# Two blocks, not three, for the experts loaded ahead of routing, and the overflow loop moved behind the 22nd expert

## What is computed

```python
def route(xt, w_router, router_bias):
    scores = jax.nn.sigmoid(jnp.dot(xt, w_router, preferred_element_type=jnp.float32))
    ...
    _, idx = lax.top_k(masked, TOP_K)          # 2 of 32 experts for each of 512 tokens
    w = jnp.take_along_axis(scores, idx, axis=-1)
    w = w / jnp.sum(w, axis=-1, keepdims=True)
    return idx, w

def moe(xt, idx, wts, w_gu, w_dn):
    ...
    def expert_block(args):
        xb, e = args
        g, u = jnp.split(xb @ w_gu[e], 2, axis=-1)
        return (jax.nn.silu(g) * u) @ w_dn[e]
    ...
    return jnp.einsum('tk,tkd->td', wts.astype(y.dtype), y)
```

## The kernel before, in words

| places | blocks each |
|---|---|
| 0 to 16 | 3 3 1 2 1 3 1 2 1 3 1 2 1 4 1 2 1 |
| 17 to 20 | 5 1 1 3 |
| 21 to 27 | 2 each |
| 28 to 31 | 1 each |

## Time and profile before

### The profile page before, as it was taken

How to read it: one execution, slowest core, us unless ns; L and a number is a source line. 1 busy time by engine, 2 the same in 40 slices (tenths; PEclk the granted TensorE clock), 3 DMA queues, 4 the chain that set the end, 5 groups by cost and what they waited for, 6 DMA issues and landing times.

```text
span 1829.8 us, 34673 instructions
## 1 busy us (share of the span) xinstructions
PE 1457.1 (80%) x14391; PEld 835.3 (46%) x14391; DVE 657.2 (36%) x1130; ACT 339.9 (19%) x776; POOL 309.1 (17%) x356
## 2 busy tenths in 40 slices
PE   3999999997985858997844999795787749888863
PEld 3644777566553424454422444344454325544431
DVE  5674777756110101111103289876311101111102
ACT  3344444111110001110102133301111001101000
POOL 1001111002221212322100111100232112222200
PEclk9998999986997979998977999896798879998976
DMA  9633222574899999999995122025699999999996
GB/s 368 241 153 147 84 80 73 160 284 190 336 393 403 404 402 363 381 408 407 411 404 216 46 75 84 3 92 230 244 371 382 408 423 358 396 409 397 415 420 243
DMA packets 89853, 517.14 MB, mean 283 GB/s; under 512 B 12859, under 2 KB 25556, under 8 KB 80242
## 3 DMA queue, kind: packets, MB, share of 16 engines
q1 hardware_dynamic: 76176, 497.96, 69.5%
q0 software_dynamic: 11616, 16.85, 2.9%
q10 hardware_dynamic: 1922, 0.29, 0.1%
HBM read 507.70 MB, written 22.02 MB: 289 GB/s over the span
## 4 chain that ended last, share of the span: by engine, by line
PE 50%; DMA 32%; DVE 11%; issue 4%; ACT 2%; SPq 1%; POOL 0%; POOLq 0%; DVEq 0%; ACTq 0%
DMA ring_gu<-in_moe_w_gu_dram 24%; PE ps L1055 15%; PE ps L1065 7%; DMA arena<-in_moe_w_gu_dram 4%; PE ps L857 3%; PE ps L972 3%; PE ps L748 3%; PE ps L884 3%; PE ps L937 2%; DVE ring_dn L1765 2%; PE ps L791 2%; PE ps L870 2%; PE ps L771 2%; PE ps L819 2%; DMA ring_gu<-in_w_ada_dram 1%
## 5 line engine op out<-in xcount | busy, mean ns | idle before, releaser
L1055 PE MATMUL ps<-ring_gu,arena 128*32 128x256 f32 x4992 | 337.4, 411 | 141.5 <-DMA ring_gu<-in_moe_w_gu_dram 92.3
L1986 DVE TENSOR_TENSOR arena<-arena,ps 128x128 f32<-128x128 f32 x120 | 34.5, 288 | 748.8 <-ACT arena L1407 748.8
L1055 PEld LDWEIGHTS ps<-ring_gu,arena 128*32 128x32 f32 x4992 | 169.9, 117 | 267.3 <-issue 94.2
L653 POOL DMA_INDIRECT ys_dram<-arena,out_idx x120 | 119.1, 992 | 750.4 <-DVE arena L1949 709.6
L1055 PE MATMUL ps<-arena 128*32 128x256 f32 x2688 | 182.7, 414 | 67.8 <-DMA arena<-in_moe_w_gu_dram 66.5
L1065 PE MATMUL ps<-ring_dn,arena 128*32 128x256 f32 x2496 | 169.6, 381 | 17.0 <-issue 13.6
L1055 PEld LDWEIGHTS ps<-arena 128*32 128x32 f32 x2688 | 90.9, 117 | 135.7 <-DMA arena<-in_moe_w_gu_dram 55.7
L1376 ACT ACTIVATE arena<-ps 128x128 f32<-128x128 f32 x120 | 33.3, 277 | 601.0 <-PE ps L1060 577.7
L646 POOL DMA_INDIRECT arena<-xn_dram,tok_idx x120 | 111.3, 927 | 116.9 <-issue 63.3
L1065 PEld LDWEIGHTS ps<-ring_dn,arena 128*32 128x32 f32 x2496 | 85.2, 110 | 85.8 <-issue 35.0
L937 PE MATMUL ps<-arena 128*128 128x512 f32 x256 | 110.6, 592 | 1.0 <-ACT arena L1189 1.0
(11 more groups left out here) (311 smaller groups left out, 1679.4 us busy)
## 6 DMA issues: line engine op xcount, KB each, us to landing
ring_gu<-in_moe_w_gu_dram SPq DMA_DIRECT2D x44, 4096.0 KB
ring_dn<-in_moe_w_dn_dram SPq DMA_DIRECT2D x44, 2048.0 KB
arena<-in_moe_w_gu_dram SPq DMA_DIRECT2D x20, 4096.0 KB
arena<-in_moe_w_dn_dram SPq DMA_DIRECT2D x20, 2048.0 KB
ring_gu<-in_w_ada_dram SPq DMA_DIRECT2D x12, 2048.0 KB, 20.4
ring_gu<-in_w_ada_dram SPq DMA_DIRECT2D x48, 512.0 KB, 3.6
arena<-in_rnn_w_in_dram SPq DMA_DIRECT2D x8, 1024.0 KB, 7.1
ring_dn<-ys_dram SPq DMA_DIRECT2D x8, 1024.0 KB, 7.9
```

What stands on the lines that cost most here:

```text
L653: g.indirect_dma_start(ys_dram, bass.IndirectOffsetOnAxis(ap=out_idx[:, col:col + 1], axis=0), yo[:, n % 4, :], None, bounds_check=2 * TIL ...
L1055: last = mm(ps[s_ * ROWS:(s_ + 1) * ROWS, pb, 0:2 * QF].rearrange("p (a b) -> p a b", a=2), rows[:, k, :], pair[:, :, s_, :], start=(k == ...
```

## The change

Experts 0 and 1 get two blocks instead of three (`CAP`, `FIXED`), and orders 18 and 19 get two blocks instead of one (`HEAVY` from 18 to 20), so that 60 blocks remain. `RUN` is written anew for these orders. The overflow loop moves from behind place 12 (block 23) to behind place 21 (block 43) and has 28 steps instead of 26. VectorE computes the new capacities with two more operations in each layer. Some small buffers in `arena` move to make room for two more columns. In the changed kernel the lines of the two products are L1056 and L1066, and those of the loop L1091 and L1092.

```diff
-MAX_EXTRA = 26
+MAX_EXTRA = 28
...
-HEAVY = 18
+HEAVY = 20
 TRIPLE = 7
-CAP = [3, 3, 5, 4, 3, 3, 3] + [2] * (HEAVY - TRIPLE) + [1] * (NE - HEAVY)
+FIXED = 2
+CAP = [2, 2, 5, 4, 3, 3, 3] + [2] * (HEAVY - TRIPLE) + [1] * (NE - HEAVY)
...
-RUN = ([0, 1, 18, 7, 19, 6, 20, 8, 21, 5, 22, 9, 23, 3, 24, 10, 25, 2, 26, 27, 4]
+RUN = ([0, 1, 20, 7, 21, 6, 22, 8, 23, 5, 24, 9, 25, 3, 26, 10, 27, 2, 4]
        + list(range(11, HEAVY)) + [28, 29, 30, 31])
...
-MORE_PLACE = 12
-MORE_UNIT = 5
+MORE_PLACE = 21
+MORE_UNIT = 10
...
-        ord_f = view(arena, 11186, NE + 1)
+        ord_f = view(arena, 5248, NE + 1)
...
                 then(v.tensor_scalar(ovb, order, float(TRIPLE), None, ALU.is_lt))
                 then(v.tensor_tensor(ncap, ncap, ovb, ALU.add))
+                then(v.tensor_scalar(ovb, order, float(FIXED), None, ALU.is_lt))
+                then(v.tensor_tensor(ncap, ncap, ovb, ALU.subtract))
```

More of the change, by code:

```diff
@@ L314, in trunk @@
         hit = arena[0:1, 9984:9984 + MAX_EXTRA * NE].rearrange("p (n e) -> p n e", n=MAX_EXTRA)
-        slot_f = view(arena, 10816, 2, NCOL)
-        slot_i = arena[:, 11036:11036 + NCOL].bitcast(I32)
-        pick8 = view(arena, 11146, 5, 2 * TT)
-        ord_f = view(arena, 11186, NE + 1)
+        slot_f = view(arena, 10880, 2, NCOL)
+        slot_i = arena[:, 11104:11104 + NCOL].bitcast(I32)
+        pick8 = view(arena, 11216, 5, 2 * TT)
+        ord_f = view(arena, 5248, NE + 1)
         stage = view(ring_gu0, 3072, 3, D)
```

## The result

The changed kernel took 1840.57 us (median of five, 1833.08 to 1842.57) against 1823.54 us for the kernel before: ratio 1.0077, 95% interval [1.0057, 1.0098], or +14.0 us (the medians alone are 17.0 apart). A second measurement beside 21 runs of the kernel before gave 1.0058 [1.0035, 1.0080], +10.6 us (medians 8.0 apart). It is slower, as forecast (+14.5); the two intervals overlap, and differences are given by the ratios from here on.

What follows compares the result with a forecast made beforehand. The prediction took the expert stages to be bound by DMA's weight transfers, TensorE mattering only when it delays a load's issue. Terms: 2 x 17.5 - 21.7 + 1.2 = +14.5 us, from 1824.5 to 1839.0 us; range 1826 to 1853.

Steps and rivals of the forecast that it cites:

- new loop: Behind the expert run as number 21: the loop's pause follows a TensorE backlog and empties DMA, losing 17.5 us a layer.
- front: Start of each layer's experts: the fourth expert's weights load is issued 10.5 us earlier, gaining 7.3 and 8.1 us.
- old gaps: Behind the loop's old position: DMA's lost transfer time disappears, gaining 3.3 us in layer 0 and 3.0 in layer 1.
- routing: Ahead of the experts: two more VectorE operations and wider comparison and sum cost 0.6 us a layer, 1.2 in all.
- Rival 2: Start of each layer's experts: the earlier load gains nothing, losing 15.4 us, so 1854 us; chance 14%.
- T: The moment the weights of the expert run as number 17 land, from which the chain to the moved loop is counted.
- three stalls: TensorE stalls in the third block of a unit, blocks 34, 38 and 42, put at 4.1 us each.
- first packets: Restart of DMA behind the new loop: their delay raised the empty stretch from 16.9 to 17.5 us a layer.
- Rival 4: Blocks 34, 38 and 42: the stalls may be absent, making the change -4.7 us, 1820 us; chance 11%.
- The rule that I had weighed: Overflow loop on TensorE: the skill's about 108 ns per compare-and-branch, against 214 traced, would make the change +2.7 us.
- Rival 5: Loop at its new place: each step misses its instructions once more at 0.8 us, 22 us a layer, 1884 us; chance 2%.
- Rival 3: The two old gaps cost more than their windows show, so nearly no change, 1827 or 1828 us; chance 13%.

Runs made afterwards that it cites:

- a_guard: The changed kernel with each engine's overflow loop inside one test for any extra blocks, so all 28 steps are skipped: 1810.78 us, 0.9925 of the kernel before.
- c_front: The changed kernel with the old order of the work and its 28-step loop back behind place 12: 1815.88 us, 0.9949 of the kernel before.
- b_guard: The kernel before with each engine's overflow loop inside one test for any extra blocks, skipping its 26 steps: 1823.93 us, 0.9983 of the kernel before.
- c_guard: The changed kernel with old order, loop behind place 12, and one test that skips the whole loop: 1813.21 us, 0.9936 of the kernel before.
- after_again: The changed kernel measured once more, with nothing altered: 1833.05 us, 1.0058 of the kernel before.
- b_loop21: The kernel before with only its 26-step overflow loop moved behind place 21 (block 43): 1827.24 us, 1.0008 of the kernel before.
- a_steps14: The changed kernel with 14 overflow-loop steps instead of 28 in all five loops: 1815.96 us, 0.9942 of the kernel before.
- before_again: The kernel before measured once more, with nothing altered: 1825.57 us, 0.9996 of the kernel before.

## Why the prediction was right, and which terms were off

The time fell into the range, by the mechanism forecast: the pause at the new place falls on a backlog and starves load 24 in both layers. The sizes were off: the loss was put 10.7 us too high and the gains, less the routing, 8.1, and the two errors nearly cancelled. That +14.5 comes so near to +14.0 and +10.6 is luck to that extent.

| term, both layers | predicted | measured |
|---|---|---|
| new loop | +35.0 | +24.5 (after less a_guard: expert stages; 24.3 by the ratios) |
| front | -15.4 | -9.3 with its routing (c_front) |
| old gaps | -6.3 | -3.1 (b_guard) |
| routing | +1.2 | in the rows above |
| sum | +14.5 | +14.0 and +10.6 |

**Front.** Right: the wait moved as said (10.9 us earlier against block 0, forecast 9 to 11), and no slice is under 250 GB/s (266 in layer 0, 251 in layer 1; the second profile has one of 248). The step that failed is "40 us at 328 instead of 401 GB/s": a front without starving runs at 376 to 389 in these profiles, not at 401. What I took for the reference was a stretch in mid-stage; with 385 in place of 401, the sum of both layers would have been about 12.6 us. c_front's gain is 9.3; the routing's 1.2, if that was as counted, and about 2 us that the gap behind place 12 took back there are already off it, so the front alone is about 12.5. That is near it. The empty stretches ahead of load 3, 6.0 + 3.0 us, are as near to the 9.3, and these runs do not tell the two ways of counting apart. Rival 2 (the front gives nothing) is refuted by c_front.

**Old gap.** The rate returned (413 and 403 GB/s), but the two gaps were worth 3.1 us, not 6.3. By the profiles it is 4.5, by c_guard against c_front 2.4, so the term is too high by 2 to 4 us.

**New loop.** The chain was T + 119.6 to block 44 and T + 120.1 to the issue. Measured: T + 117.1 and T + 117.6 in layer 0, and 116.4 to the issue in layer 1 (1675.03 less T = 1558.67). Two of the three stalls were there; block 42's was not (6.45 us, where block 38 took 9.25), and that is the 2.5 us. DMA ran dry at T + 103.1 in layer 0, for a forecast of 103.2, and 2.1 us after the forecast in layer 1 (T + 105.3). So the empty stretches were 15.4 and 12.0 instead of 16.9 us each. The loss, 24.5 for 27.4 us of empty queue, is 0.9 of it, and the 0.6 us a layer that I had added for the first packets does not show. Rival 4 (faster, without stalls) had a third of its premise: it needed a chain under 113 us.

**Block 42's stall.** The traces together tell when it is absent. In the seven profiles with the loop elsewhere TensorE waits 1.1 to 2.7 us for issue behind block 42's transposes, in both layers; in the five with the loop right behind block 43 (after, after_again, b_loop21, a_guard, a_steps14) it waits in none of the ten layers (once, in layer 0 of b_loop21, the block follows a wait of 1.05 us for its weights). Block 22 is alike: no stall where the loop stands behind block 23 (before, before_again, b_guard, c_front, c_guard), 1.56 us in both layers of b_loop21, where it does not. TensorE's timeline at block 42 of before, and at block 22 of b_loop21:

```profile
802.63 1.10 PE L1065 MATMUL ps<-arena 128*32 128x256 f32 x6 [0.81 <-issue]
804.07 0.86 PE L1065 MATMUL ps<-arena 128*32 128x256 f32 x11 [0.34 <-issue]
```

```profile
631.80 0.64 PE L1065 MATMUL ps<-arena 128*32 128x256 f32 x4 [0.79 <-issue]
633.21 0.44 PE L1065 MATMUL ps<-arena 128*32 128x256 f32 x3 [0.77 <-issue]
```

So the unit that ends in the loop runs without its stall, even where the steps are skipped (a_guard): moving the loop behind block 43 took the stall of block 42 with it. Why, no run shows.

**The step of the loop.** The rule that I had weighed is settled by two readings. The branches at the new place took 214 ns in the median of 56, and the second one of each step 218 ns. And 14 steps less took 10.6 us from TensorE's idle time, 0.76 us a step. The Trainium skill (Advanced Engine Details and Errata, Control Flow Timing) gives about 108 ns for a compare-and-branch. An estimate by that figure had put the change near +2.7 us, and the traces, with 214 and 218 ns and a loss of 24.3 us at the new place, do not agree. Rival 5 (each step fetches its instructions anew, +22 us a layer) is refuted by the same median and by the pause of 24.57 us. The longest branch was 1647 ns, and nothing like 0.8 us came on top of each of the 28 steps. The line of the second branch in the changed kernel:

```profile
L1091 PEldq COMPARE_BRANCH  x56: 86/218/242, 805.4 to 1674.0; - x56
```

**Rival 3** (nearly no change, because the two old gaps cost more than they show) is refuted: they cost less.

**The sum.** The loop's 24.3 less a_guard's 13.7 gives back the +10.6, but that tests nothing, as a_guard stands on both sides. A sum of parts measured by themselves is 24.3 - 9.3 (c_front) - 3.1 (b_guard) = +11.9, beside +10.6 and +10.7 (expert stages). The first measurement gave +14.0; the 3.4 us between the two are within their intervals, and their mix of short and long executions goes the same way. **Open** stays what makes the long ones; why the stall is absent in the unit that ends in the loop; and why the stages ahead of the experts end anywhere from 446.4 to 455.2.

## What to carry to other kernels

A loop that runs nothing is not free: here 28 skipped steps held TensorE for 21 us, and one test around the whole loop took all but 3 us of the pause away, which gave the changed kernel 24 us, more than any other place for the loop did. A pause of an engine that releases buffers cost here about what it exceeds the loads in flight by; before moving it, count the time from the last landing to the next issue against the transfers queued, with the backlog of the places ahead of it. When a stretch is starved, do not take the rate that it would otherwise reach from the best stretch of the stage: the front, once it no longer starved, ran at 376 to 389 GB/s, not at 401.

## What the hardware showed that was not expected

- A compare-and-branch of this loop is 214 ns on TensorE's queue and 45 ns on SyncE's, a fifth. The whole skipped step, from one branch to the same one of the next step, differs far less: in the changed kernel the median is 0.74 us on TensorE's, 0.53 on VectorE's, 0.50 on SyncE's and 0.44 on ScalarE's and GpSimd's. So a step is more than its branches, and TensorE is the slowest of the five. In the trace of the kernel before, the line of SyncE's loop (count, min/median/max ns):

```profile
L530 SPq COMPARE_BRANCH  x52: 40/45/45, 648.5 to 1503.9; - x52
```

- Fully busy DMA moves 376 to 389 GB/s at the front, where the stage's first loads are started, and 398 to 413 in the mid-stage windows shown, with a share of 1.00 to 1.02 in both. What makes the difference no run shows.
- TensorE's wait for issue of some 3 us in the third block of a unit, in rows like that of 767.88, comes in most units that run without a wait and is absent in the one that ends in the loop, and in block 54 where that runs without a wait (after, b_loop21 and a_steps14). The rows mark only a part of it as idle: 1.48 of the 2.8 us at block 38. a_guard has it right behind its 3.19 us pause as well.
